# A seventh-product scheme with eight quads a column pair instead of seven, one weight sum of each made by an adding transfer

## The reference

```python
h = layer_norm(x, emb_ln_g, emb_ln_b)                       # 256 x 4096
proj = h @ w_in                                             # 4096 columns in, all branches' columns out
q_a, kv_a, dq, dk, dv, g_mla, g_dswa, r_mla, r_dswa = split(proj)
a = mla_attention(q_a, kv_a, ...)                           # q_a: 1024 columns, the latent queries
y_mla  = (a * silu(g_mla)) @ w_o_mla
y_dswa = (dilated_mixture(dq, dk, dv, rel_bias) * silu(g_dswa)) @ w_o_dswa
out = (sigmoid(r_mla) * y_mla + sigmoid(r_dswa) * y_dswa) @ w_out
return layer_norm(ALPHA * h + out)
```

## Time and profile before

| | |
|---|---|
| median of three runs | 2694.84 us (2694.43 to 2696.74) |
| the profiled execution | 2694.9 us span; its own device time is that span |
| PE busy | 2662.6 us, 99% |
| DVE busy | 2019.2 us, 75% |
| ACT busy | 1286.9 us, 48% |
| POOL busy | 128.5 us, 5% |
| bytes moved | 568.59 MB, 211 GB/s |
| granted PE clock | 0.997 of full speed |

### The profile page before, as it was taken

The page is one execution under the profiler, slowest core; times in us unless marked ns, Lnnn a source line. Parts: engine busy times, 40 slices in busy tenths (PEclk is TensorE's granted clock), DMA queues, the critical chain, the costliest instruction groups (busy, mean ns, idle before and its releaser), DMA issues.

```text
span 2694.9 us, 32634 instructions
## 1 busy us (share of the span) xinstructions
PE 2662.6 (99%) x12402; PEld 2221.2 (82%) x12402; DVE 2019.2 (75%) x1975; ACT 1286.9 (48%) x1259; POOL 128.5 (5%) x211
## 2 busy tenths in 40 slices
PE   7999999999999999999999999999999999999998
PEld 5988888888888888888888889988888888888886
DVE  7778888888888888988888867765565566656557
ACT  5444554444444454555555555554454444433333
POOL 0000000000000000000000001110010100100000
PEclk9999999999999999999999999999999999999998
DMA  6666666665666656666666664357776777776765
GB/s 206 191 212 220 207 220 208 222 217 197 227 220 214 224 186 235 216 224 218 214 208 219 220 206 140 121 166 207 243 236 182 233 222 236 244 230 222 229 217 177
DMA packets 217224, 568.59 MB, mean 211 GB/s; under 512 B 14953, under 2 KB 31701, under 8 KB 217092
## 3 DMA queue, kind: packets, MB, share of 16 engines
q1 hardware_dynamic: 198992, 506.51, 57.0%
q0 software_dynamic: 16880, 57.85, 6.9%
q10 hardware_dynamic: 1224, 2.44, 0.2%
HBM read 540.46 MB, written 26.29 MB: 210 GB/s over the span
## 4 chain that ended last, share of the span: by engine, by line
PE 91%; DVE 5%; DMA 3%; ACT 1%; issue 1%; SPq 0%; DVEq 0%; ACTq 0%
PE acc L594 13%; PE acc L596 13%; PE acc L595 13%; PE bank L614 4%; PE bank L619 4%; PE bank L618 4%; PE acc L614 4%; PE acc L618 4%; PE acc L619 4%; DMA q_raw<-in_w_in 2%; PE acc L603 2%; PE acc L601 2%; PE acc L602 2%; PE bank L656 2%; PE bank L657 2%; PE bank L653 2%
## 5 line engine op out<-in xcount | busy, mean ns | idle before, releaser
L1005 ACT ACTIVATE q_hi<-q_raw 128x2048 fp32r<-128x2048 f32 x272 | 521.4, 1917 | 649.9 <-DVE q_raw L1284 298.5
L1290 DVE TENSOR_TENSOR q_low<-q_raw,q_hi 128x2048 fp32r<-128x2048 f32 x272 | 619.3, 2287 | 158.0 <-ACT q_hi L1005 158.0
L1207 DVE TENSOR_TENSOR w_lo<-w_raw,w_hi 128x1024 fp32r<-128x1024 f32 (+2 forms) x448 | 504.5, 1139 | 298.0 <-ACT w_hi L964 294.9
L964 ACT ACTIVATE w_hi<-w_raw 128x1024 fp32r<-128x1024 f32 (+2 forms) x448 | 431.6, 983 | 302.8 <-PE acc L596 262.6
L594 PE MATMUL acc<-w_hi,oper_hi 128*128 128x512 f32 (+1 forms) x1072 | 410.0, 382 | 0.3 <-DVE w_lo L1207 0.3
L596 PE MATMUL acc<-w_hi,oper_lo 128*128 128x512 f32 (+1 forms) x1072 | 405.7, 378 | 0.0
L595 PE MATMUL acc<-w_lo,oper_hi 128*128 128x512 f32 (+1 forms) x1072 | 405.3, 378 | 0.0
L594 PEld LDWEIGHTS acc<-w_hi,oper_hi 128*128 128x128 f32 x1072 | 201.3, 188 | 37.7 <-DVE w_lo L1207 1.5
L596 PEld LDWEIGHTS acc<-w_hi,oper_lo 128*128 128x128 f32 x1072 | 201.2, 188 | 37.3
L595 PEld LDWEIGHTS acc<-w_lo,oper_hi 128*128 128x128 f32 x1072 | 201.4, 188 | 36.1
L618 PE MATMUL bank<-q_hi,oper_hi 128*128 128x512 f32 x576 | 224.1, 389 | 0.0
(11 more groups left out here) (341 smaller groups left out, 4333.8 us busy)
## 6 DMA issues: line engine op xcount, KB each, us to landing
q_raw<-in_w_in SPq DMA_DIRECT2D x256, 1024.0 KB, 4.9
w_raw<-in_w_in SPq DMA_DIRECT2D x128, 512.0 KB, 4.4
w_raw<-in_w_out SPq DMA_DIRECT2D x128, 512.0 KB, 3.8
w_raw<-in_w_o_mla SPq DMA_DIRECT2D x64, 512.0 KB, 4.7
q_raw<-in_w_in SPq DMA_DIRECT2D x32, 512.0 KB, 4.6
w_raw<-in_w_o_dswa SPq DMA_DIRECT2D x32, 512.0 KB, 4.1
w_raw<-in_w_q_b SPq DMA_DIRECT2D x32, 384.0 KB, 3.5
w_raw<-in_w_in SPq DMA_DIRECT2D x32, 288.0 KB, 3.2
```

Of the source, the lines that this page charges most:

```text
L964: act.activation(w_hi[:, n % RING, 0:w], w_raw[:, n % RING, 0:w], ACT.Copy).then_inc(w_hi_ready, 1)
L1005: act.activation(q_hi[h][:, 0:4, :], q_raw[r][:, :, :], ACT.Copy).then_inc(q_hi_ready, 1)
L1207: dve.tensor_tensor(w_lo[:, n % RING, 0:w], w_raw[:, n % RING, 0:w], w_hi[:, n % RING, 0:w].bitcast(F32), ALU.subtract).then_inc(w_lo_read ...
L1290: dve.tensor_tensor(q_low[r], q_raw[r], q_hi[h][:, 0:4, :].bitcast(F32), ALU.subtract).then_inc(q_lo_ready, 1)
```

## The change

One more quad of each pair is made with seven products: `SEVEN` becomes 2, 4, 5, 7, 9, 11, 13, 14. The scheme is written with other signs so that one of the four weight sums is lower left plus lower right of the quad, and stands in place of a raw tile. This sum is made by an adding transfer: when the raw quad has landed, POOL issues a transfer that reads the tile of 128x512 once more from DRAM and adds it to the raw tile (`first_sum`). DVE is left with one sum of 512 columns and one of 1024. ACT's first `quad_high` waits for the adding transfer, no longer for DVE's sums. Six raw buffers take the place of four. The sixth lies where `qa_sb` is, so the latent queries are stored to DRAM behind DVE's copy, and loaded again when the last quad in that buffer has been read; quad 5's load waits for the store. The stores of a pair's results are issued behind the adding transfer of q = 9 of the next pair. `T_STEPS` has eight places, four of them in section part `qa0`. POOL's descriptor space is cut from its default to 4096 bytes a partition, which makes room.

```diff
-SEVEN = tuple(range(2, QUADS - 1, 2))
+SEVEN = (2, 4, 5, 7, 9, 11, 13, 14)
-RAWS, HIS = 4, 3
+RAWS, HIS = 6, 3
+QA_RAW = RAWS - 1
-T_STEPS = (("qa0", 6), ("qa0", 10), ("qa0", 14), ("kva0", 4), ("kva0", 8), ("kva0", 12), ("kva1", 12))
+T_STEPS = (("qa0", 5), ("qa0", 8), ("qa0", 11), ("qa0", 14), ("kva0", 4), ("kva0", 8), ("kva0", 12), ("kva1", 12))
@@ SP, quad_loads
+                    elif g == QA_RAW:
+                        sp.wait_ge(qa_stored, 16)
@@ ACT, quad_high
                 if is_seven(g):
-                    act.wait_ge(sums_ready, sevens_before(g) + 1)
+                    act.wait_ge(s1_made[r], first_sums(g))
                 else:
                     act.wait_ge(q_loaded[r], quad_arrivals(g))
                 act.activation(q_hi[h][:, 0:4, :], q_raw[r][:, :, :], ACT.Copy).then_inc(q_hi_ready, 1)
                 if is_seven(g):
+                    act.wait_ge(sums_ready, sevens_before(g) + 1)
@@ DVE, quad_sums
-                dve.wait_ge(q_loaded[r], quad_arrivals(g))
+                dve.wait_ge(s1_made[r], first_sums(g))
                 if m >= 2:
                     before = [n for n in range(g) if is_seven(n)][-2]
                     dve.wait_ge(quad_done, before + 1)
-                a21 = raw[:, 1:2, :].broadcast_to([P, 2, CW])
-                dve.tensor_tensor(out_[:, 0:2, :], a21, raw[:, 3::-3, :], ALU.add).then_inc(sum_step, 1)
-                dve.wait_ge(sum_step, 2 * m + 1)
-                dve.tensor_tensor(out_[:, 2, :], out_[:, 0, :], raw[:, 0, :], ALU.add).then_inc(sum_step, 1)
-                dve.wait_ge(sum_step, 2 * m + 2)
-                dve.tensor_tensor(raw[:, 1, :], out_[:, 2, :], raw[:, 2, :], ALU.add).then_inc(sums_ready, 1)
+                dve.tensor_tensor(out_[:, 0, :], raw[:, 1, :], raw[:, 0, :], ALU.subtract).then_inc(sum_step, 1)
+                dve.wait_ge(sum_step, m + 1)
+                s2 = out_[:, 0:1, :].broadcast_to([P, 2, CW])
+                dve.tensor_tensor(out_[:, 1:3, :], raw[:, 3:1:-1, :], s2, ALU.subtract).then_inc(sums_ready, 1)
@@ POOL
-            for p in range(PAIRS):
+            def first_sum(g):
+                raw = q_raw[g % RAWS]
+                pool.wait_ge(q_loaded[g % RAWS], quad_arrivals(g))
+                p, q = g // QUADS, g % QUADS
+                below = w_in[0][(2 * q + 1) * P:(2 * q + 2) * P, BLOCK_COLS[2 * p + 1]:BLOCK_COLS[2 * p + 1] + CW]
+                pool.dma_start(raw[:, 1, :], below, accum_op=ALU.add).then_inc(s1_made[g % RAWS], 16)
+            for g in range(NQ):
+                if is_seven(g):
+                    first_sum(g)
+                if g == SEVEN[0]:
+                    pool.wait_ge(acc_free, 4)
+                    pool.dma_start(qa_d[:, :, :], qa_sb[:, :, :]).then_inc(qa_stored, 16)
+                if g >= QUADS and g % QUADS == SEVEN[4]:
+                    store_pair(g // QUADS - 1)
+            last_user = NQ - 1 - (NQ - 1 - QA_RAW) % RAWS
+            pool.wait_ge(raw_free, last_user - last_user // QUADS)
+            pool.dma_start(qa_sb[:, :, :], qa_d[:, :, :]).then_inc(qa_loaded, 16)
+            store_pair(PAIRS - 1)
```

More of the change, by code:

```diff
@@ L106, in quad_arrivals, with first_sums @@
     return 16 * sum(len(pair_loads(n // QUADS)) for n in range(g % RAWS, g + 1, RAWS))
+def first_sums(g):
+    return 16 * sum(is_seven(n) for n in range(g % RAWS, g + 1, RAWS))
 def gated_pieces(p):
@@ L299, in program @@
     gated_mla_d = nc.dram_tensor("gated_mla", (D // CW, P, TT, CW), F32).ap()
+    qa_d = nc.dram_tensor("latent_queries", (P, TT, Q_RANK), F32).ap()
     bias_rows_d = nc.dram_tensor("bias_rows", (NG * GH, PITCH), F32).ap()
@@ L328, in program @@
         t_hi = sb("t_hi", R_A, [P, len(SEVEN), 4, P], F32R)
[L329 to L333, removed]
+        t_lo = sb("t_lo", R_A + 16 * K, [P, len(SEVEN), 4, P], F32R)
+        h_pair = sb("h_pair", R_A + 32 * K, [P, 2, SEQ])
+        t_val = sb("t_val", R_A + 34 * K, [P, 4, P])
+        q_raw = [sb(f"q_raw{n}", at_, [P, 4, CW]) for n, at_ in enumerate((R_B, R_B + 8 * K, RINGS + 32 * K, RINGS + 40 * K, R_D, R_C + 24 * K))]
+        q_low = [sb(f"q_low{n}", at_, [P, 4, CW], F32R) for n, at_ in enumerate((R_B, R_B + 8 * K, RINGS + 32 * K, RINGS + 40 * K, R_D, R_C + 24 * K))]
         q_hi = [sb(f"q_hi{n}", at_, [P, 7, CW], F32R) for n, at_ in enumerate((R_C, RINGS, RINGS + 14 * K))]
-        q_sum = [sb(f"q_sum{n}", R_C + 32 * K + 3328 + n * 6 * K, [P, 3, CW]) for n in range(2)]
-        q_sum_low = [sb(f"q_sum_low{n}", R_C + 32 * K + 3328 + n * 6 * K, [P, 3, CW], F32R) for n in range(2)]
-        c_first = sb("c_first", R_A + 28 * K, [P, 2, CW])
+        q_sum = [sb(f"q_sum{n}", SMALL + 3328 + n * 6 * K, [P, 3, CW]) for n in range(2)]
+        q_sum_low = [sb(f"q_sum_low{n}", SMALL + 3328 + n * 6 * K, [P, 3, CW], F32R) for n in range(2)]
+        c_first = sb("c_first", R_A + 32 * K, [P, 2, CW])
         c_sb = [c_first[:, 0, :], c_first[:, 1, :], sb("c_third", R_C + 14 * K, [P, CW]), sb("c_fourth", RINGS + 28 * K, [P, CW])]
@@ L649, in seven_quad @@
                 pe.wait_ge(q_lo_ready, splits_before(g) + 1)
-                four = ((p1, oper_hi[:, k1, tok(0)], oper_lo[:, k1, tok(0)]), (p3, oper_hi[:, k2, tok(1)], oper_lo[:, k2, tok(1)]),
+                four = ((p1, oper_hi[:, k1, tok(0)], oper_lo[:, k1, tok(0)]), (p5, t_hi[:, n, 0, :], t_lo[:, n, 0, :]),
                         (p2, oper_hi[:, k2, tok(0)], oper_lo[:, k2, tok(0)]), (p4, t_hi[:, n, 3, :], t_lo[:, n, 3, :]))
                 for m, (y, b_hi_, b_lo_) in enumerate(four):
-                    ins = pe.matmul(y, b_hi_, raw_lo[:, m, :], start=m == 0 and first, stop=False)
+                    ins = pe.matmul(y, b_hi_, raw_lo[:, m, :], start=m < 2 and first, stop=False)
                 ins.then_inc(raw_free, 1)
@@ L656, in seven_quad @@
                     pe.matmul(y, b_hi_, hi[:, m, :], start=False, stop=False)
-                    pe.matmul(y, b_lo_, hi[:, m, :], start=False, stop=m == 0 and last)
+                    pe.matmul(y, b_lo_, hi[:, m, :], start=False, stop=m < 2 and last)
                 pe.wait_ge(q_lo_ready, splits_before(g) + 2)
-                three(p5, t_hi[:, n, 0, :], t_lo[:, n, 0, :], hi[:, 4, :], sum_lo[:, 0, :], first, last)
+                three(p6, t_hi[:, n, 2, :], t_lo[:, n, 2, :], hi[:, 4, :], sum_lo[:, 0, :], first, last)
                 three(p7, t_hi[:, n, 1, :], t_lo[:, n, 1, :], hi[:, 5, :], sum_lo[:, 1, :], first, last)
-                three(p6, t_hi[:, n, 2, :], t_lo[:, n, 2, :], hi[:, 6, :], sum_lo[:, 2, :], first, last).then_inc(quad_done, 1)
+                three(p3, oper_hi[:, k2, tok(1)], oper_lo[:, k2, tok(1)], hi[:, 6, :], sum_lo[:, 2, :], False, False).then_inc(quad_done, 1)
             def column_pairs():
```

24 lines of the change are left out of this document (15 added, 9 removed).

## The result

The changed kernel takes 2698.9 us (median of 20 runs, 2696.8 to 2701.3), the kernel before 2695.5 (20 runs, 2694.4 to 2697.3): ratio 1.0013, 95% interval 1.0007 to 1.0019. That is 3.4 us slower, inside the bound of 0.2% in which the prediction called a time unchanged. The most likely forecast was 2686.3 us, 0.3% faster; the measured time lies inside the range of 2680 to 2700 us, near its dear end, and the gain isn't there.

The account below looks back on a forecast made before the run. The prediction took the kernel as bound by PE's matmul count, DVE close behind. It summed 2694.9 - 11.6 - 7.3 + 1.6 + 2.5 + 5.9 + 0.3 = 2686.3 us, range 2680 to 2700.

Parts of the forecast that it names:

- Matmuls, -11.6: In 17 pairs, one direct quad becomes a seven-product one: 3 matmuls fewer each, 51 in all, 11.6 us less PE time.
- Waits at q = 5, -7.3: At q = 5 in the pairs, PE's waits of 0.66 us a pair, 7.3 over eleven, should go.
- DVE in time at the double quads: At q = 4, 5 and 13, 14, DVE's low parts come in time, 1 us spare; narrowest at q = 6, 0.3 spare.
- Token sums in `start`, +1.6: In `start`, four places three slots apart make PE wait at `w_lo`, together 1.6 us; bounds 0 and 2.5.
- First pair, q = 1, +2.5: Before q = 1 of the first pair, PE waits 2.5 us for quad 2's adding transfer, DVE's sums and low part.
- the adding transfer's 3.7: Time from issue to landing assumed for an adding transfer, 3.7 us, that of a 512 KB load by the same queue.
- Its upper bound of 7.4: Dearest time allowed for an adding transfer, that of a 512 KB store beside loads; 2.3 us was the lower bound.
- First pair, q = 4, +5.9: Before q = 4 of the first pair, PE waits 5.9 us behind latent-query store, quad 5's load, adding transfer and DVE.
- q = 6, +0.3: At q = 6 of the first pair, behind the stall, doubled low parts make PE late once by 0.3 us.
- the first pair costs more: Rival, chance 0.20: waits in each pair stay or the first pair is dearer, so 7.3 us are not won: 2693.6.
- Too long for its lead: Rival, chance 0.17: adding transfers outlast their 11 to 14 us of room, PE waits in every pair: 2720 to 2770.
- Two of the signs on record: Adding transfers landing in 3 to 5 us would confirm; a latent-query store far from 7 us would show it wrong.

Follow-up runs that it names:

- e11: Changed kernel with all first sums on DVE, token sums four slots apart, five raw buffers, latent queries kept in SBUF: 2678.1 us, 0.9938 of the kernel before.
- e15: Changed kernel with all first sums on DVE, token sums four slots apart, four raw buffers, latent queries kept in SBUF: 2687.6 us, 0.9971 of the kernel before.
- e7: Changed kernel with all 136 first sums made by DVE, no adding transfer: 2681.6 us, 0.9951 of the kernel before.
- after: The profiled execution of the changed kernel itself: span 2696.8 us, time 2698.6 us.
- e12: Changed kernel with loads of quads 3 and on held until the first adding transfer has landed: span 2692.8 us, one execution.
- e1: Changed kernel with plain transfers in place of the 136 adding ones, first weight sum left out: span 2691.7 us, one execution.
- e2: Changed kernel with the first sums of quads 2, 4 and 5 of the first pair on DVE: 2682.2 us, 0.9952 of the kernel before.
- e16: Changed kernel with plain transfers for adding ones, and loads of quads 3 and on held until the first has landed: span 2688.8 us, one execution.

## Why the prediction was wrong

In its own steps, span against span:

- **Matmuls, -11.6.** Right: 12351, periods of 81.60.
- **Waits at q = 5, -7.3.** Right in place and size (7.4). Runs e11 and e15 show that it needs a fifth buffer; that the order of ACT and DVE alone would do is refuted. Whether the buffer would do without the new order no run shows.
- **DVE in time at the double quads.** Right, and with more room than thought: e7 adds 5.5 us a pair and loses nothing in nearly all pairs. I counted slack at PE's need and did not see that the idle time ahead of the sums (126 us in 14 pairs of after) is free for one more operation on the raw quad.
- **Token sums in `start`, +1.6.** Two gaps of 0.66 us at the places named; PE was behind by 1.7 us across them. Right. Another 0.7 came from the first loads and 0.3 from small gaps.
- **First pair, q = 1, +2.5.** The mechanism was right, the size not: 6.7. All of the 4.2 us too few are one term, the adding transfer's 3.7, measured at 7.9. **This is the step that failed**, and it fails again at q = 4, where it is 4.5 short. The 3.7 was taken from a 512 KB load by the same queue, the median of seven plain transfers (3.4 to 5.2 us). These had loads beside them too, of 512 KB, issued 0.9 and 2.0 us behind them. Here two of 1 MB are issued within 0.6 us of it, and it adds: alone it takes 4.3 us (e12), plain in the same company 5.6 (e1). Its upper bound of 7.4 was a store "beside loads", the nearer row for a transfer beside loads, and I put it down as a bound only.
- **First pair, q = 4, +5.9.** Measured 8.8, through larger errors that partly cancel: the store 4.4 (6.8 forecast), the load 8.1 (4.9), the adding transfer 8.2 (3.7): +5.3, less 2.1 by which PE itself was late from the slow matmuls behind q = 1 and a gap at q = 3, and 0.3 in hand-overs. Two overlaps were put at nothing here. The adding transfer of quad 4, named as standing behind the store, lengthened quad 5's load by about 3 us: without it the load takes 5.0 (e2, e7), as it does with a plain one (5.2 in e1, 5.0 in e16). The loads of quads 6 to 8, named as queued behind SP's wait, land on top of quad 5's adding transfer: even a plain one takes 6.4 us there (e1, e16), against 2.9 alone. Releasing a queue is a burst.
- **Missing: the clock.** The sum has nothing for matmuls after a stall; they cost 3.7 us.
- **q = 6, +0.3.** Not there: DVE had it back.
- **Behind the pairs.** 1.35 us less than before from q = 15 of the last pair to the end, in gaps that move from run to run.

Together, measured less forecast: 4.2 (q = 1) + 2.9 (q = 4) + 3.7 (clock) + 0.4 (the gap at q = 3) + 0.7 (loads) + 0.4 (`start`) - 0.3 (q = 6) - 0.3 (steady pairs) - 1.35 = 10.4 of 10.5.

Of the rivals, "the first pair costs more" is what happened, beyond the size it was given: 8.7 us were forecast for that pair, 19.6 came, of stalls and clock. "Too long for its lead" did not: 5.7 us median inside the pairs against a room of 11 to 14. Two of the signs on record did show: adding transfers of 5.8 us in the median where 3 to 5 were named, and a store of the latent queries of 4.4 us, far from 7. What the prediction did not weigh is the plainest rival: that the adding transfer is not needed, since DVE has the time.

## What to carry to other kernels

Price a transfer by the company it will have: at a start or behind a released wait, list everything that is issued within its flight, with its size and its distance, and take the row of a transfer in such a crowd. Where none exists, the dearer bound is the better term: here the row on record of a store beside loads (7.4) was near the 7.9 measured. Before work is moved from an engine to the DMA queues, look for that engine's idle time just ahead of the operation: waiting for a buffer leaves room to prepare its input. And a stall of several us on PE cost another 1.6 to 2.9 us in slow matmuls each time here.
